# Input projection in two passes of four tiles, cache copies beside the first, samples routed from group 23

## The chip, the cores and the metric

The kernel runs on one core of one Trainium2 chip. The metric is the device time of one execution in microseconds (us), from the first to the last instruction with what lies around it; lower is better. Before the change it is 3765.6 us, the median of three runs (3765.25 to 3778.32).

## What is computed

One layer of a hybrid decoder, on 1024 prompt tokens and 64 sample tokens (8 sequences of 8), all in fp32, model width 1024:

```
z   = x @ w_in                      # 1024 x 2560: q, k, v, GLU value a, GLU gate g, 512 columns each
att = dilated sliding-window attention(q, k, v)      # 8 heads of 64
cnv = swish(LayerNorm(causal depthwise conv(a * sigmoid(g), width 31)))
x1  = LayerNorm(ALPHA * x + concat(att, cnv) @ w_out)
# PEER: 8 heads, query of 256, two sides of 128 keys
s   = (x1 @ w_query) against sub_keys;  top 16 of each side, top 16 of their 256 sums -> 128 experts per token
y   = LayerNorm(ALPHA * x1 + sum_k gate_k * gelu(x1 . expert_u[e_k]) * expert_v[e_k])
```

The samples attend to a cache of 2048 rows. The outputs also hold the new keys, values and GLU rows, and both caches (keys and values of 8 sequences) shifted by 8 rows, which are plain copies from DRAM to DRAM.

## The kernel before

**Tiles and stages.** The tokens are 9 tiles: 0 to 7 of 128 prompt tokens, and tile 8 (`PT`) of the 64 samples. Each engine runs its own hand-written program over stages `n` from -1 to 10; a stage has 32 groups `g`, a group four quarters `i`. In stage `n` the *front* of tile `m = n+1` runs (projection of later tiles, attention in groups 0 to 9, convolution, output projection in 11 and 12, LayerNorm in 13 and 14, queries, key scores and routing of 8 PEER heads from group 15 on), beside the *dots* of tile `n` (each: one gather of `expert_u` rows for 128 tokens by POOL, L574, and one multiply-and-sum on DVE, L1039) and the *values* of tile `n-1` (one gather of `expert_v` rows per token, L589, and four matmuls of it, L1376). A gather moves 512 KB. A dot of stage -1 can be made early, between the routing of heads of tile 0: 56 are (`EARLY_AT`); the other 72 of tile 0 are spread over stage 0. POOL runs no further ahead than its rings: 6 buffers for u, 8 for v.

**Routing.** One head is a fixed run of small DVE operations on 128 rows (`route_side` twice, `route_pairs`, `route_experts`). For prompt tiles head `h` begins at quarter 69 + 7h of the stage (group 17.25). For the samples (stage 7) head `h` takes the four quarters of group 24 + h; their queries and key scores run in groups 22 to 29.

**Projection.** `w_in` is read in steps of 128 columns (a, g four times, then k, q four times) and two v steps of 256 columns. Three passes go over all 18 steps (`PASSES`): the 128 tokens of tile 0; 512 tokens; the last 384 tokens with the 64 samples beside them (448 columns). A *unit* is 8 matmuls for one step (for v: one step and one tile). The profile shows each fp32 matmul as two records, so a unit is x16. Pass 0 (18 units, banks in rotation of 8) stands alone ahead of stage -1; the 24 units of pass 1 lie in stage -1 and the 24 of pass 2 in stage 0, in the groups that a table names, each behind the front's work of its group on PE:

```
UNIT_GROUP = [[2, 5, 8, 11, 14, 15] + [16 + j * 15 // 18 for j in range(18)], [j * 31 // 24 for j in range(24)]]
```

ACT copies each unit out of PSUM (`evacuate`) and then issues the weight load (L640, L642) of the step that takes the slot next (`w_ring`, 4 slots of 512 KB). Behind a g unit DVE multiplies a by sigmoid(g) (`gated`, L885) at the start of the next group, and ACT stores the product a group later (`gated_store`). In pass 0 q, the GLU rows and k of tile 0 stay in SBUF; later tiles go through scratch in DRAM. POOL's first value gather waits for all units, since the v ring lies where x and the weights lay.

**Queues.** SP issues, in this order: the first weights and x, constants; behind the third step from the end of pass 0 x of pass 1, `w_out`, the keys and LayerNorm rows; the first 8 cache copies (L458, 4080 KB each), the first near the end of pass 0 and one more after each head of stage -1; x of pass 2; the loads of front 1; the other 8 copies, one per head of stage 0; in stage 1 the projected outputs. A load of `wq` (1 MB per head) is issued by ACT.

**Value groups.** `v_group_at` (L425) makes the values of tile `n-1` run two groups behind (`V_LAG`), and `LAG` (L124) makes the 64 dots of the samples in stage 8 begin at group 2.

```
            k = GROUPS * (n - 1) + g - V_LAG
            return divmod(k, GROUPS) if 0 <= k < GROUPS * TILES else None
```

In stage 7 the samples' attention takes groups 0 to 17, their convolution rows 16 to 18, the output projection group 19, LayerNorm groups 20 and 21.

Of the kernel before, what the change touches and what calls it, by code (L numbers as in the profile page):

```python
# [10 lines left out]
ALU = mybir.AluOpType  # L11
# [3 lines left out]
P = 128  # L15
# [21 lines left out]
PH = 8  # L37
# [27 lines left out]
PASSES = ((0, P, 0), (P, 512, 0), (5 * P, 3 * P, NS))  # L65
# [3 lines left out]

def pass_tiles(p):
    t0, tn, sn = PASSES[p]
    return [(t0 + tn) // P - tn // P + j for j in range(tn // P)] + ([PT] if sn else [])
# [7 lines left out]

UNITS = []
for _p in range(3):
    for _s, (_k, _i) in enumerate(STEPS):
        UNITS += [(_p, _s, _k, _i, _t) for _t in (pass_tiles(_p) if _k == "v" else [None])]
UNIT_AT = [sum(1 for _u in UNITS if _u[0] < _p) for _p in range(4)]
FIRST_LOADS = UNIT_AT[1] - 6

def evac_ops(u):  # L90
    p, _, kind, _, _ = UNITS[u]
    return 2 if p == 2 and kind in "kq" else 1
# [7 lines left out]
for _p in range(3):  # L100
# [9 lines left out]
def unit(p, kind, i):  # L110
    return max(n for n, u in enumerate(UNITS) if u[0] == p and u[2:4] == (kind, i))

# [3 lines left out]
UNIT_GROUP = [[2, 5, 8, 11, 14, 15] + [16 + j * 15 // 18 for j in range(18)], [j * 31 // 24 for j in range(24)]]  # L116
assert all(len(UNIT_GROUP[p]) == UNIT_AT[p + 2] - UNIT_AT[p + 1] for p in range(2))
GATE_GROUP = [[UNIT_GROUP[p][2 * i + 1] for i in range(CT)] for p in range(2)]
# [5 lines left out]
LAG = 2  # L124
# [3 lines left out]

def units_at(m, g):  # L130
    return [UNIT_AT[m + 1] + j for j, at_ in enumerate(UNIT_GROUP[m]) if at_ == g] if m < 2 else []
# [41 lines left out]
def build(nc, I, O):  # L173
# [6 lines left out]
    with ctx:  # L180
# [85 lines left out]
        idf = small([P, SLOTS])  # L266
        dots = [small([P, SLOTS]) for _ in range(2)]
# [13 lines left out]
        assert base + taken[0] <= nc.sbuf_usable_end, (base + taken[0], nc.sbuf_usable_end)  # L281
# [6 lines left out]
        xT = [at(o_ring, [P, KD, P])] + [at(o_ring + U_RING * D * 4, [P, KD, 512])] * 2  # L288
# [7 lines left out]
        vs = at(o_l + 2 * D * 4 + 3 * 512 * 4, [NS, AW])  # L296
        conv_new = at(o_l + 2 * D * 4, [P, CT, NS])

# [18 lines left out]
        past_out = sem("past_out")  # L317
# [84 lines left out]
        q_free = {(p, i): 16 * (2 * (p - 1) + i // 2) for p in (1, 2) for i in range(CT)}  # L402
        glu_free = {(1, 0): 0, (1, 1): 0, (1, 2): 0, (1, 3): 16, (2, 0): 32, (2, 1): 16, (2, 2): 16, (2, 3): 80}
        GLU_FOUR, GLU_ALL = (32, 16, 16), (128, 64, 64)
# [19 lines left out]

        def v_group_at(n, g):  # L425
            k = GROUPS * (n - 1) + g - V_LAG
            return divmod(k, GROUPS) if 0 <= k < GROUPS * TILES else None
# [10 lines left out]
        def _(sp):  # L438
            sp.dma_start(w_ring[:, 0, :, :], I["w_in_t"][0]).then_inc(w_in_s[0], 16)
            sp.dma_start(xT[0][:, :, :], I["xT"][:, :, 0:P]).then_inc(xT_in[0], 16)  # L440
# [8 lines left out]
            sp.dma_start(xT[1][:, :, :], I["xT"][:, :, P:P + 512]).then_inc(xT_in[1], 16)  # L449
# [20 lines left out]
            def projected_loads():  # L470
                sp.wait_ge(proj_done, UNIT_AT[2])
                sp.dma_start(xT[2][:, :, 0:3 * P + NS], I["xT"][:, :, 5 * P:TOK]).then_inc(xT_in[2], 16)

            def projected_stores():
                sp.wait_ge(proj_evac, EVACS[-1])
                sp.dma_start(vs_o, vs[:, :]).then_inc(vs_out, 16)
                sp.dma_start(kT_o, kT[:, :, :]).then_inc(st_out, 16)
# [4 lines left out]
            def front_loads(m):  # L482
# [6 lines left out]
                if m == 1:  # L489
                    sp.wait_ge(past_out, 16)  # L490
# [70 lines left out]
            for i in range(3):  # L561
                sp.wait_ge(glu_out[i], GLU_ALL[i])
# [974 lines left out]
```

## Time and profile before

| | us |
|---|---|
| median of three runs | 3765.6 |
| the profiled execution, its own time | 3800.66 |
| span of the profiled execution | 3798.8 |

| engine | busy us | share |
|---|---|---|
| PE | 2453.4 | 65% |
| DVE | 2527.9 | 67% |
| POOL | 2128.8 | 56% |
| ACT | 387.7 | 10% |

The DMA engines moved 1394.91 MB, 367 GB/s over the span; the gathers' queue has 1140.99 MB of it. In the page's slices the DMA engines are busy 90% and more nearly everywhere, and TensorE's clock moves between its two levels. Times in the trace are counted from the span's start. A share of busy time is an average over stages with different limits, so the stretches are to be read one by one: in each, which wait ends last. The chain of waits names for each stretch the work that the rest waited for.

### The profile page before, as it was taken

The numbers are of one execution on the slowest core, as the hardware profiler recorded it, in microseconds if no ns is written. First come the engines' busy times: TensorE is split into PE (matmuls) and PEld (weight loads), VectorE is DVE, ScalarE is ACT, GpSimd is POOL, SyncE is SP. The second block draws the span as 40 slices with busy tenths as digits, with TensorE's granted clock in tenths as the row PEclk, the third lists the DMA queues.
The fourth block names the chain that finished last, engine by engine and source line by source line (L and its number), as shares of the span: only waits on it lengthen the run. The fifth ranks groups of instructions, "written<-read, shape, count | busy, mean of one in ns | idle before, by whom it ended". The sixth has DMA issues, their size and how long they took to land.

```text
span 3798.8 us, 32774 instructions
## 1 busy us (share of the span) xinstructions
PE 2453.4 (65%) x10596; PEld 1095.8 (29%) x10596; DVE 2527.9 (67%) x6632; ACT 387.7 (10%) x753; POOL 2128.8 (56%) x2180
## 2 busy tenths in 40 slices
PE   7894792666557655665666676767665655655558
PEld 5462371223123312222323132314231222321112
DVE  5288589768866886588668875887587434683331
ACT  2111211100110011001110011002100111000000
POOL 0042224666666665666566656666666545647665
PEclk8897895678668866887687767877787777778899
DMA  9998988999999998999899989999999999979998
GB/s 340 354 340 307 398 322 309 372 384 383 363 353 395 408 354 331 393 410 361 322 386 411 367 334 377 410 366 363 367 410 388 412 415 403 372 287 375 361 367 319
DMA packets 375450, 1394.91 MB, mean 367 GB/s; under 512 B 44712, under 2 KB 55592, under 8 KB 362856
## 3 DMA queue, kind: packets, MB, share of 16 engines
q0 software_dynamic: 313344, 1140.99, 78.4%
q1 hardware_dynamic: 40384, 143.03, 10.1%
q10 hardware_dynamic: 21552, 108.79, 7.4%
q8 instruction: 86, 1.41, 0.1%
q14 instruction: 84, 0.69, 0.0%
HBM read 1379.40 MB, written 80.18 MB: 384 GB/s over the span
## 4 chain that ended last, share of the span: by engine, by line
DVE 34%; PE 16%; issue 15%; POOL 14%; DMA 12%; another core or an unknown queue 7%; ACT 2%; ACTq 0%; SPq 0%; DVEq 0%; POOLq 0%
DVE t L1039 14%; POOL t L589 8%; DMA t<-in_expert_v,t 6%; PE psum L1376 6%; POOL t L574 6%; DMA t<-in_expert_u,t 5%; PE psum L1233 4%; DVE t L987 2%; DVE t L985 2%; DVE t L900 2%; DVE t L988 2%; DVE t L986 2%; PE psum L1277 1%; PE psum L1253 1%
## 5 line engine op out<-in xcount | busy, mean ns | idle before, releaser
L1376 PE MATMUL psum<-t,t 128*32 128x512 f32 x4352 | 1264.4, 782 | 797.5 <-DMA t<-in_expert_v,t 584.5
L574 POOL DMA_INDIRECT t<-in_expert_u,t x1088 | 1062.9, 977 | 976.0 <-DVE t L1039 510.3
L589 POOL DMA_INDIRECT t<-in_expert_v,t x1088 | 1065.6, 979 | 675.5 <-issue 298.1
L1039 DVE CUSTOM_DVE_ANT_0 t<-psum,t 128x1024 f32<-128x1024 f32 x928 | 1116.8, 1220 | 337.9 <-DMA t<-in_expert_u,t 294.4
L1376 PEld LDWEIGHTS psum<-t,t 128*32 128x32 f32 x4352 | 258.2, 129 | 1608.0 <-issue 1536.9
L1332 PE MATMUL psum<-t,t 128*128 128x128 f32 (+1 forms) x2304 | 302.5, 292 | 34.4 <-issue 22.9
L1332 PEld LDWEIGHTS psum<-t,t 128*128 128x128 f32 x2304 | 291.2, 207 | 87.2 <-issue 72.8
L1039 DVE CUSTOM_DVE_ANT_0 t<-t,t 128x1024 f32<-128x1024 f32 x160 | 194.3, 1223 | 155.6 <-DMA t<-in_expert_u,t 153.8
L1233 PE MATMUL psum<-t,t 128*128 128x128 f32 (+2 forms) x768 | 258.8, 496 | 7.0 <-DMA t<-in_xT 6.3
L900 DVE SCALAR_TENSOR_TENSOR t<-t,t,t 128x128 f32<-128x128 f32 x840 | 237.8, 345 | 0.5 <-issue 0.4
L1253 PE MATMUL psum<-t,t 64*128 64x512 f32 (+3 forms) x192 | 119.7, 748 | 100.2 <-issue 53.4
L1277 PE MATMUL psum<-t,t 128*128 128x64 f32 x576 | 106.8, 350 | 112.3 <-issue 99.1
L1233 PEld LDWEIGHTS psum<-t,t 128*128 128x128 f32 x768 | 132.6, 203 | 118.4 <-issue 111.2
L1277 PEld LDWEIGHTS psum<-t,t 128*128 128x128 f32 x576 | 98.4, 259 | 184.9 <-issue 165.6
L1313 PE MATMUL psum<-t,t 128*128 128x512 f32 (+1 forms) x288 | 134.0, 620 | 3.4 <-ACT t L694 3.4
L1055 DVE SCALAR_TENSOR_TENSOR t<-t,t 128x128 f32<-128x128 f32 (+1 forms) x288 | 80.5, 281 | 83.4 <-PE psum L1376 55.9
L984 DVE MAX8 t<-t 128x8 f32<-128x128 f32 (+3 forms) x216 | 72.3, 335 | 94.2 <-ACT t L738 57.2
L730 ACT ACTIVATE t<-psum 128x256 f32<-128x256 f32 (+1 forms) x72 | 26.7, 371 | 882.1 <-remote 788.0
L1344 PE MATMUL psum<-t,t 128*128 128x128 f32 (+1 forms) x288 | 63.8, 359 | 79.2 <-ACT t L730 46.6
L933 DVE CUSTOM_DVE_ANT_0 t<-psum,t 128x128 f32<-128x128 f32 (+7 forms) x64 | 48.1, 752 | 97.1 <-PE psum L1253 47.0
L1344 PEld LDWEIGHTS psum<-t,t 128*128 128x128 f32 (+1 forms) x288 | 49.6, 237 | 145.7 <-issue 73.5
L1039 DVE DVE_READ_ACCUMULATOR2_ANT t<- 128x1 f32 x1088 | 89.5, 82 | 0.0
(140 smaller groups left out, 1805.7 us busy)
## 6 DMA issues: line engine op xcount, KB each, us to landing
t<-in_wq_t ACTq DMA_DIRECT2D x72, 1024.0 KB
out<-in_cache_k_win SPq DMA_DIRECT2D x8, 4080.0 KB
out<-in_cache_v_win SPq DMA_DIRECT2D x8, 4080.0 KB
t<-in_w_in_t ACTq DMA_DIRECT2D x44, 512.0 KB, 8.0
t<-in_kc_t SPq DMA_DIRECT2D x8, 2560.0 KB, 15.1
t<-in_vc_t SPq DMA_DIRECT2D x8, 2560.0 KB
t<-in_expert_u,t POOLq DMA_INDIRECT x1088
t<-in_expert_v,t POOLq DMA_INDIRECT x1088
```

Of the source, the lines that this page charges most:

```text
L574: pool.indirect_dma_start(u_buf[:, k % U_RING, :], None, I["expert_u"][0], bass.IndirectOffsetOnAxis(ap=idn[t % 2][:, s:s + 1], axis=0)).t ...
L589: pool.indirect_dma_start(v_buf[:, k % V_RING, :], None, I["expert_v"][0], bass.IndirectOffsetOnAxis(ap=idT[t % 3][:, tau:tau + 1], axis=0 ...
L900: dve.scalar_tensor_tensor(dst, src, w, dst, ALU.mult, ALU.add).then_inc(cv, 1)
L1039: dve.tensor_tensor_reduce(out=u_buf[:, k % U_RING, :], in0=x1P if banked else x1[t % 3][:, :], in1=u_buf[:, k % U_RING, :], scale=1.0, sc ...
L1055: dve.scalar_tensor_tensor(zt[:, k % Z_RING, 0:w, :], iota[:, :].unsqueeze(1).broadcast_to([P, w, 32]), float(g), c3, ALU.is_equal, ALU.mu ...
L1233: last = pe.matmul(dst[:, 0:tn + sn], w_ring[:, r, k, :], xT[p][:, k, 0:tn + sn], start=(k == 0), stop=(k == KD - 1))
L1253: last = pe.matmul(bank[2 + half][:, 0:w], qT[r:r + E, c, :], kT[r:r + E, c, half * 512:half * 512 + w], start=True, stop=True)
L1277: last = pe.matmul(bank[2][:, 0:E], pT[:, j * P:(j + 1) * P], v[:, j, h * E:(h + 1) * E], start=(j == 0), stop=(j == m))
L1313: last = pe.matmul(bank[3 - half][0:rows(m), :], mixedT[:, k, 0:rows(m)], w_out[:, k, half * 512:(half + 1) * 512], start=(k == 0), stop=( ...
L1332: last = pe.matmul(bank[2 + h % 2][:, side * r:(side + 1) * r], wq[:, h % 2, k, side * KEYC:(side + 1) * KEYC], x1T[:, k, 0:r], start=(k = ...
L1344: last = pe.matmul(bank[4 + h % 2][0:r, side * NK:(side + 1) * NK], qh[:, h % 2, side * r:(side + 1) * r], skT[:, 2 * h + side, :], start= ...
L1376: last = pe.matmul(bank[half][32 * j:32 * j + 32, :], zt[:, (GROUPS * t + g) % Z_RING, j, :], v_buf[:, k % V_RING, half * 512:(half + 1) * ...
```

## The change

**Two passes.** `PASSES = 2`, each of 512 tokens (four tiles). Pass 0 has 24 units (16 of 512 columns, 8 v units) and still stands ahead of stage -1. In pass 1 each a, g, k and q step is two units, one of 512 columns and one of the 64 samples, whose x has a buffer of its own (`xTs`, on the place of tile 7's v; so the last v unit of tile 7 goes to the end); with v 42 units, in groups 4 to 52 counted from the start of stage -1. The weights are read twice, not three times.

**Tile 0's rows.** In pass 0 ACT writes q twice (tile 0's part to `qT`, all to the store), DVE multiplies the GLU rows of tile 0 a second time into `gl`, and all four tiles go to scratch; the store of tile 0's last 30 rows goes away. The samples' GLU rows are made in place in `gluS` and stored from there by SP in stage 1.

**Copies.** Nine of the 16 cache copies are issued beside pass 0 (after units 4, 6, ... 20), four in stage -1, three in stage 0. x of pass 1 is issued by ACT behind its last work of pass 0.

**Samples.** Their queries begin at group 21 and head `h` of their routing at quarter 92 + 9h/2 (group 23 on); the first LayerNorm operations move two quarters up. `HOLD, HELD`: in groups 18 and 19 of stage 7 no value group runs, and from there the values are four groups behind. `LAG` is 4. The value stream ends at group 3 of stage 10, and the last LayerNorm follows it there.

```diff
-PASSES = ((0, P, 0), (P, 512, 0), (5 * P, 3 * P, NS))
+HALF = SEQ // 2
+HT = HALF // P
+PASSES = 2
...
+        _tiles = range(HT * _p, HT * (_p + 1)) if _k == "v" else [None]
+        _tiles = ([PT] if _p and _k == "v" else []) + list(_tiles) + ([PT] if _p and _k != "v" else [])
+        UNITS += [(_p, _s, _k, _i, _t) for _t in _tiles]
...
+FIRST_LOADS = 2
+COPY_AT = [4, 6, 8, 10, 12, 14, 16, 18, 20]
...
-UNIT_GROUP = [[2, 5, 8, 11, 14, 15] + [16 + j * 15 // 18 for j in range(18)], [j * 31 // 24 for j in range(24)]]
-GATE_GROUP = [[UNIT_GROUP[p][2 * i + 1] for i in range(CT)] for p in range(2)]
+STEP_GROUP = [4, 8, 12, 15, 17, 19, 21, 23, 25, 27, 29, 31, 33, 36, 39, 42]
+UNIT_GROUP = [_g for _g in STEP_GROUP for _ in range(2)] + [43 + _j for _j in range(10)]
+GATE_GROUP = [STEP_GROUP[2 * _i + 1] for _i in range(CT)]
...
-LAG = 2
+LAG = 4
...
+HOLD, HELD = GROUPS * (PT - 2) + 18, 2
+SAMPLE_ROUTE = [92 + 9 * _h // 2 for _h in range(8)]
+SAMPLE_QUERY = 21
...
+        def v_number(n, g):
+            at_ = GROUPS * (n - 1) + g
+            if HOLD <= at_ < HOLD + HELD:
+                return None
+            return at_ - V_LAG - (HELD if at_ >= HOLD else 0)
...
-            for i in range(PH):
-                if i:
-                    sp.wait_ge(sm_done, i)
-                else:
-                    sp.wait_ge(proj_done, UNIT_AT[1] - 2)
+            for i, u in enumerate(COPY_AT):
+                sp.wait_ge(proj_done, u)
                 copy_cache(i)
...
-            projected_loads()
+            for i in range(4):
+                sp.wait_ge(sm_done, 2 * i + 1)
+                copy_cache(len(COPY_AT) + i)
...
+            act.dma_start(xT[:, :, :], I["xT"][:, :, HALF:SEQ]).then_inc(xT_in[1], 16)
...
+                if p == 0:
+                    step(dve.tensor_tensor(gl[:, i, PAST:], dst[:, 0:P], gate[:, 0:P], ALU.mult))
+                dve.tensor_tensor(dst, dst, gate, ALU.mult).then_inc(glu_done, 1)
+                if p:
+                    dve.wait_ge(proj_evac, EVACS[unit(p, "g", i, PT)])
+                    dve.tensor_tensor(gluS[:, i, :, PAST:], gluS[:, i, :, PAST:], sigS[:, i % 2, :].rearrange("p (b t) -> p b t", b=NB),
+                                      ALU.mult).then_inc(gluS_done, 1)
...
-                if g >= 24:
-                    if i < 2:
-                        route_side(PT, g - 24, i)
-                    elif i == 2:
-                        route_pairs(PT, g - 24)
-                    else:
-                        route_experts(PT, g - 24)
+                for h in range(PH):
+                    at_ = 4 * g + i - SAMPLE_ROUTE[h]
+                    if at_ in (0, 1):
+                        route_side(PT, h, at_)
+                    if at_ == 2:
+                        route_pairs(PT, h)
+                    if at_ == 3:
+                        route_experts(PT, h)
...
+                if u == UNIT_AT[1] + 1:
+                    pe.wait_ge(xT_in[2], 16)
...
+                if tile is None:
+                    x_, w = xT, HALF
+                elif tile < PT:
+                    x_, w = xT[:, :, (tile - HT * p) * P:(tile - HT * p + 1) * P], P
+                else:
+                    x_, w = xTs, NS
```

Where the instructions stand, at three places. First PE at the start of stage -1: L1253 (L1291 in the changed kernel) are the scores of a head, L1266 (L1304) the transposes of its weights, L1277 (L1315) its values, L1233 (L1271) a projection unit; t_122 and, in the changed kernel, t_121 are x, t_123 the weights. Before:

```order
L1253 MATMUL psum<-t_50,t_53 128x128 [waits const_in,proj_evac]
L1266 MATMUL psum<-t_94,t_56 128x128 [waits exp_done]
L1253 MATMUL psum<-t_50,t_53 128x128 [waits sm_done]
L1277 MATMUL psum<-t_51,t_57 128x64 [waits sm_done,pT_ready]
L1266 MATMUL psum<-t_94,t_56 128x128 [waits pT_ready,exp_done]
L1253 MATMUL psum<-t_50,t_53 128x128 [waits att_done,sm_done]
L1233 MATMUL psum<-t_122,t_123 128x512 [waits proj_evac,w_in0,xT_in1]
```

The changed kernel, from the fourth head's scores on:

```order
L1291 MATMUL psum<-t_50,t_53 128x128 [waits att_done,sm_done]
L1315 MATMUL psum<-t_51,t_57 128x64 [waits att_done,sm_done,pT_ready]
L1304 MATMUL psum<-t_94,t_56 128x128 [waits pT_ready,exp_done]
L1291 MATMUL psum<-t_50,t_53 128x128 [waits att_done,sm_done]
L1271 MATMUL psum<-t_121,t_123 128x512 [waits proj_evac,w_in0,xT_in1]
L1271 MATMUL psum<-t_121,t_123 128x512 x7
L1271 MATMUL psum<-t_122,t_123 128x64 [waits proj_evac,w_in0,xT_in2]
L1271 MATMUL psum<-t_122,t_123 128x64 x7
L1315 MATMUL psum<-t_51,t_57 128x64 [waits att_done,sm_done,pT_ready]
```

The first unit stood behind the scores of the third head; now it stands behind those of the fifth, and a unit of 64 columns with the same weights follows it. Second, PE in the first groups of stage 0. Before, a unit follows the scores in each of these groups:

```order
L1253 MATMUL psum<-t_50,t_53 128x256 [waits att_done,sm_done]
L1233 MATMUL psum<-t_122,t_123 128x448 [waits proj_evac,w_in1]
L1233 MATMUL psum<-t_122,t_123 128x448 x7
L1277 MATMUL psum<-t_51,t_57 128x64 [waits att_done,sm_done,pT_ready]
L1277 MATMUL psum<-t_51,t_57 128x64
L1266 MATMUL psum<-t_94,t_56 128x128 [waits pT_ready,exp_done]
L1266 MATMUL psum<-t_94,t_56 128x128
L1253 MATMUL psum<-t_50,t_53 128x256 [waits att_done,sm_done]
L1233 MATMUL psum<-t_122,t_123 128x448 [waits proj_evac,w_in2]
```

The changed kernel:

```order
L1271 MATMUL psum<-t_121,t_123 128x512 [waits proj_evac,w_in0]
L1271 MATMUL psum<-t_121,t_123 128x512 x7
L1271 MATMUL psum<-t_122,t_123 128x64 [waits proj_evac,w_in0]
L1271 MATMUL psum<-t_122,t_123 128x64 x7
L1315 MATMUL psum<-t_51,t_57 128x64 [waits att_done,sm_done,pT_ready]
L1315 MATMUL psum<-t_51,t_57 128x64
L1304 MATMUL psum<-t_94,t_56 128x128 [waits pT_ready,exp_done]
L1304 MATMUL psum<-t_94,t_56 128x128
L1291 MATMUL psum<-t_50,t_53 128x256 [waits att_done,sm_done]
L1315 MATMUL psum<-t_51,t_57 128x64 [waits att_done,sm_done,pT_ready]
```

Two heads in three now have no unit behind their scores, and the third has two units. Third, POOL in stage 7, the changed kernel around the held groups (L601 gathers u, L616 v; before, u and v take turns there):

```order
L601 DMA t_86<-in_expert_u,t_96 128x1024 [waits a_dot]
L616 DMA t_87<-in_expert_v,t_99 128x1024 [waits pv]
L601 DMA t_86<-in_expert_u,t_96 128x1024 [waits a_dot] x8
L601 DMA t_86<-in_expert_u,t_96 128x1024 [waits a_dot,a_route]
L616 DMA t_87<-in_expert_v,t_99 128x1024 [waits pv_first]
```

Eight v gathers are gone from between the u gathers; they come after the rest of the stream, in stage 8.

## Rows read from the trace of the kernel before

**Rows 1.** The page: its first line, one group of gathers, one group of loads

```profile
span 3798.8 us, 32774 instructions
...
L574 POOL DMA_INDIRECT t<-in_expert_u,t x1088 | 1062.9, 977 | 976.0 <-DVE t L1039 510.3
...
t<-in_w_in_t ACTq DMA_DIRECT2D x44, 512.0 KB, 8.0
```

**Rows 2.** Windows: us from:to, length, busy of five engines, clock, DMA share, GB/s

```profile
54.00:178.00 124.00, 99.18 (x265) 49.88 (x265) 21.80 (x70) 28.39 (x61) 0.00 (x0) 0.83 1.02 352
178.00:334.00 156.00, 113.90 (x505) 77.80 (x504) 139.35 (x387) 13.94 (x32) 58.57 (x62) 0.88 0.89 319
334.00:495.00 161.00, 127.07 (x360) 67.05 (x360) 95.02 (x260) 33.66 (x69) 39.24 (x40) 0.86 1.00 382
495.00:617.00 122.00, 78.73 (x432) 62.00 (x430) 114.49 (x348) 15.76 (x39) 31.31 (x34) 0.83 0.78 284
1400.00:1800.00 400.00, 244.02 (x1024) 102.53 (x1023) 294.30 (x769) 39.78 (x74) 255.47 (x264) 0.77 0.97 374
```

**Rows 3.** Chain of waits, 0 to 200 us (start us, us, what)

```profile
6.29 5.48 PE psum L1233 x32
...
65.77 9.78 PE psum L1233 x16
...
98.36 8.70 PE psum L1233 x16
...
123.19 6.87 PE psum L1233 x16
130.06 6.88 PE psum L1313 x16
...
143.10 1.97 PE psum L1321 x8
...
178.57 0.22 DVE t L984
...
188.37 0.18 DVE t L1016
```

**Rows 4.** Timeline of PE, 40 to 200 us (start us, us, what, idle before)

```profile
49.62 3.72 PE L1231 MATMUL psum<-t,t 128*128 128x256 f32 x16 [1.15 <-DMA t<-in_w_v_t]
53.81 0.48 PE L1253 MATMUL psum<-t,t 64*128 64x128 f32 x2 [0.47 <-ACT t L614]
```

**Rows 5.** Chain of waits, 333 to 620 us

```profile
334.59 1.12 DVE t L897 x4
...
386.14 1.09 PE psum L1277 x4
...
393.21 1.08 PE psum L1277 x4
...
429.26 0.44 PE psum L1294 x4
...
495.54 0.30 DVE t L984
...
616.53 1.12 DVE t L897 x4
```

**Rows 6.** DMA issues, all of the run: count, KB each, median us to landing

```profile
t<-in_xT SPq DMA_DIRECT2D x1, 2048.0 KB, 15.4
t<-in_xT SPq DMA_DIRECT2D x1, 1792.0 KB, 19.2
```

**Rows 7.** Timeline of PE at 3271 us, queries of the 64 samples

```profile
3271.51 6.09 PE L1332 MATMUL psum<-t,t 128*128 128x64 f32 x47
```

**Rows 8.** Windows of the samples' routing

```profile
3260.00:3300.00 40.00, 27.88 (x157) 17.65 (x158) 16.46 (x40) 1.31 (x4) 24.62 (x25) 0.71 0.99 375
3340.00:3380.00 40.00, 23.54 (x120) 11.20 (x120) 37.66 (x118) 1.31 (x4) 21.30 (x23) 0.77 0.89 323
3400.00:3420.00 20.00, 7.02 (x34) 1.54 (x34) 13.95 (x42) 4.42 (x7) 3.78 (x5) 0.59 0.28 98
```

More of the change, by code:

```diff
@@ L99 @@
 _uses, _last = [0] * 4, [None] * 4
-for _p in range(3):
+for _p in range(PASSES):
     for _s, _slots in enumerate(STEP_SLOTS):
@@ L476, in projected_stores @@
                 sp.dma_start(vs_o, vs[:, :]).then_inc(vs_out, 16)
+                sp.wait_ge(gluS_done, CT)
+                for c in range(CT):
+                    sp.dma_start(glus_o[:, c, :].rearrange("p (b t) -> p b t", b=NB), gluS[:, c, :, PAST:]).then_inc(glus_out, 16)
                 sp.dma_start(kT_o, kT[:, :, :]).then_inc(st_out, 16)
@@ L519, in cache_copies @@
             def cache_copies():
-                for h in range(PH):
-                    sp.wait_ge(sm_done, PH + h + 1)
-                    copy_cache(PH + h)
+                for i in range(len(COPY_AT) + 4, 2 * NB):
+                    sp.wait_ge(sm_done, PH + 2 * (i - len(COPY_AT) - 4) + 1)
+                    copy_cache(i)
             def store_y(t):
@@ L801, in sample_front @@
                     x1_transposed(PT)
-                if 22 <= g < 30:
-                    for h in (g - 22 - g % 2, g - 21 - g % 2):
-                        if g % 2:
-                            score_copy(PT, h)
-                        else:
-                            query_copy(PT, h)
+                heads, second = sample_heads(g)
+                for h in heads:
+                    if second:
+                        score_copy(PT, h)
+                    else:
+                        query_copy(PT, h)
                 if g == 31:
@@ L848, in _ @@
                         sample_front(g)
-                    if n == -1 and g == 1:
-                        act.wait_ge(glu_done, CT)
-                        act.dma_start(glu_d[:, :, P:P + PAST], gl[:, :, P:P + PAST]).then_inc(past_out, 16)
-                    if n < 1:
-                        for i in range(CT):
-                            if g == GATE_GROUP[m][i] + 2:
-                                gated_store(m + 1, i)
+                    for i in range(CT):
+                        if GROUPS * m + g == GATE_GROUP[i] + 2:
+                            gated_store(1, i)
                     for u in units_at(m, g):
@@ L1440, in sample_front @@
                     x1_transposes(PT)
-                if 22 <= g < 30:
-                    for h in (g - 22 - g % 2, g - 21 - g % 2):
-                        if g % 2:
-                            key_scores(PT, h)
-                        else:
-                            queries(PT, h)
+                heads, second = sample_heads(g)
+                for h in heads:
+                    if second:
+                        key_scores(PT, h)
+                    else:
+                        queries(PT, h)
             def front(m, g):
```

148 lines of the change are left out of this document (71 added, 77 removed).

## The prediction

> **What bounds the kernel now.** I read the page first, then windows by stage, then the chain of waits at their borders, then PE's timeline where the chain ran through projection units. The page gives the span, 3798.8 us, and the two gather streams of 1088 gathers each [rows 1]; the windows show four stretches ahead of a long steady part, cut at events of the chain:
>
> - 0 to 53.8: pass 0 alone. PE's first scores start at 53.81, right behind the last v unit [rows 4].
> - 53.8 to 178.6 (124.8 us): front of tile 0, until DVE starts the first head's routing [rows 3]. PE is busy 99 of 124 us, DVE 22 [rows 2], and the chain goes through units [rows 3].
> - 178.6 to 334.6 (156.0): routing with early dots, up to the first taps of stage 0 [rows 3, 5]. DVE is busy 139 of 156: DVE bounds it [rows 2].
> - 334.6 to 495.5 (160.9): front of tile 1 until its routing [rows 5]. PE 127 of 161, DVE 95 [rows 2].
> - 495.5 to 616.5 (121.0): its routing and the remaining dots; DVE 114 of 122, DMA share only 0.78 [rows 2, 5].
> - 616.5 on: one gather of u and one of v per token slot. DMA share 0.97 at 374 GB/s, no engine above 74% [rows 2]. This is bound by DMA, and its DMA work is the same in both kernels, except for where the samples' end leaves gaps.
>
> So the DMA engines are full on average, but ahead of 616.5 the chain does not run through them: the share is 1.02 at 54 to 178 because copies were put there, not because someone waits for them. From this follows my reading: the time is the moment at which stage 1 can start, plus a fixed DMA-bound rest. Copies must only be out of the way by then.
>
> **Part 1, pass 0 (+100 us).** Before, its end is at 53.8. Now: the first matmul starts at 6.3 with 1 MB loaded [rows 3]; 1.5 MB more of x at 352 GB/s [rows 2] adds 4.5, so 10.8. 16 units of 512 columns at 6.87 us, measured where PE ran without a break [rows 3]: 110. Eight v units at 3.72 [rows 4]: 30. The first v load can be issued only behind unit 13, about 14 us before it is needed; I allow 3. Sum 153.8, against 53.8: +100. Beside it lie nine copies and the constants. Weights have four slots, 27 us ahead, against 8.0 us median to landing [rows 1], and 76 GB/s of demand: hidden, if the copies do not crowd them out (rival below). The doubled q copies (ACT) and GLU products (DVE) are 0.4 to 0.7 us beside units of 6.87: nothing. DVE's 124 taps for tile 0 move under pass 0.
>
> **Part 2, front of tile 0 (-29).** Before 124.8 with nine units in groups 2 to 16. Now four steps (groups 4, 8, 12, 15), each 6.87 us plus a unit of 64 columns. The row for 64 columns is 47 records in 6.09 us, 130 ns each, so 16 records are 2.1 us [rows 7]; a step is 9.0. After attention pauses a 512-column unit took 9.78 and 8.70 instead of 6.87 [rows 3], so 2 more at groups 4 and 8. Heads without a unit go at some 2.2 us (an estimate: 124.8 less nine units and the pieces below leaves about that). Step by step: five heads 10; wait for x of pass 1, whose 2048 and 1792 KB took 15.4 and 19.2 us to land [rows 6] and which is issued when pass 0 ends: 17 less 10 is 7; step 11; four heads 9; step 11; from the end of group 8's unit (107.0) to the x1 transposes (143.1) before took 36, one unit of 6.87 in it [rows 3]: the unit at group 12 now covers the LayerNorm gap of 6.2 (136.9 to 143.1) and costs 9.0, so 32; transposes 2; queries 3.6; step 9; sigmoid and product 1.3, for which DVE waits in group 16 ahead of the routing. Sum 96: -29. Ends for this part: -40 (x lands in time, no slow units) and -10 (x 15 us late, units at half clock).
>
> **Part 4, front of tile 1 (-24).** Before 160.9. Group pitch with no unit is 7.07 us (386.14 to 393.21), DVE's own pace [rows 5]. Now group 0 has no unit but DVE's work keeps it at 13; groups 1, 4, 7: 2.9 of attention plus 9.0, 11.9 each; groups 2, 3, 5, 6 at 7.07. Sum 77 to group 8, before 95 (334.59 to 429.26 [rows 5]). Groups 8 to 17 before took 66. Now: convolution LayerNorm uncovered 8, its neighbours 1, step 9, two halves of the output projection 14, seven v units, 26 less the 6 that the LayerNorm gap hides, transposes, scores and copies 3: 55, and queries 3.6: 59. With 1 us of slow clock in all: 137. -24. The GLU products leave this stage; in it DVE waited for units that are in the sum already. Ends: -36 and -10.
>
> **Part 5, routing of tile 1 (0)**: DVE-bound with DMA idle a fifth of the time, before and after. The 10.5 MB of weights saved and five copies fewer in stage 0 fall into DMA time that nobody waits for: nothing. If stage 0 were DMA-bound, 10.5 MB at 374 GB/s would be 28 us (rival).
>
> **Part 6, samples (-9).** At 3300 to 3410 DVE is busy 37.7 of 40 us [rows 8]: eight heads at about 10 us (178.57 to 188.55 [rows 3]) plus four dots each. DMA falls to 0.89 and, at 3400 to 3420, to 0.28 while PE waits in order for the last routing [rows 8]. Lost there: about 20 us of DMA time in all. Head 0 moves into group 23, which DMA bounds, so the DVE-bound stretch is a head shorter: -9. The eight held v gathers make groups 18 and 19 shorter by 11 us (8 times 0.524 MB at 374 GB/s) and are paid again in stage 8, where DMA is full: zero. They do not lift PE's wait for the last head. `LAG` 4 moves dots within a DMA-bound stage: zero. Ends: -20 (all lost DMA time) and +6 (with the holds, DVE waits for the output projection while only u gathers are under way).
>
> **Sum.** 100 - 29 - 24 - 9 = +38. The profiled execution took 3800.66 us, 35 above the median 3765.6; I carry the difference over: 3803.6, rounded 3803 (+1.0%).
>
> **Rivals.**
> - *DMA decides after all (faster).* If the stretches up to 616 are paced by DMA (share 1.02 and 1.00 in two of four [rows 2]), copies put under a PE-bound pass and 10.5 MB less pay: -28 from the bytes and -9 at the end, about 3729. It decides if heads and units in 54 to 178 waited for loads. Against it: the chain there alternates PE and DVE, and the window's PE is busy 80%. Chance 0.12.
> - *Most of the pass is won back (no change).* x lands in time (-7), no slow units (-5), first gathers at once (-6), stage 0 at its lower end (-12), all idle DMA time at the samples filled (-11): +38 becomes about -3, and around half of these gives +15. 3765 to 3782. Chance 0.17.
> - *Copies crowd out the weights (slower still).* By 154 us the kernel now wants 62 MB (nine copies of 4.18, weights 11.5, output weights and keys 7, x 2.4, stores and small ones 3.5); at 352 GB/s [rows 2] that takes 176. If the weights wait their turn by bytes, pass 0 ends at 176: +22, 3825; with x of pass 1 late as well, 3835. For it: the sum of bytes. Against it: beside running copies weights landed in 8.0 us median [rows 1]. The Trainium skill, "DMA: Bandwidth & Descriptors", section Queues, rings and completion order, says each engine takes turns between queues by packet, which would keep ACT's weights moving past SP's backlog; by that rule this rival gets less. Chance 0.14.
> - That the samples' stream or the copies are not moved as said: the order of instructions leaves no room for that.
>
> **Chances.** Forecast 0.57, its own range 3784 to 3822. About 0.5%, 19 us, is what a measurement of this kernel can tell from no change. Faster by more: 0.12, the first rival. Within: 0.17 of the second and 0.01 of the forecast's edge, 0.18. Slower: 0.70. The range takes in the second and most of the third rival and a part of the first: 3752 to 3832.
>
> **What would show it.** Right: first scores at 150 to 157 us, PE without gaps before; first u gather (before at 188.8, right behind the first head [rows 3]) at 250 to 265; first taps of stage 1 at 655 to 675 instead of 616.5; steady stages unchanged; DMA share in the second tile's front well under 1. DMA at the samples' end still with one hole of some 15 us. Wrong: taps of stage 1 ahead of 630 (parts 2 and 4 won more), or scores behind 165 (crowding), or steady stages of another length, which would mean that the rest was not fixed.

## The result and the profile after

The changed kernel takes 3821.6 us (median of four runs, 3819.95 to 3831.56) against 3772.0 for the kernel before in the same comparison: ratio 1.0133, interval 1.0109 to 1.0157. It is 49.6 us slower. Forecast were 3803 and +38, range 3752 to 3832.

The profiled execution of the changed kernel took 3819.95 us, 19 more than that of before (3800.66). The medians differ by 50; so the profiled pair shows 30 us less than the medians, a difference between two executions and not of the change: the profiled execution of before is itself 29 us above the median of its kernel. Where it sits is seen when the span is cut at the events of the prediction. The page first, its first line and the DMA volume:

```profile
span 3818.1 us, 32732 instructions
...
DMA packets 375914, 1384.89 MB, mean 363 GB/s; under 512 B 48504, under 2 KB 56312, under 8 KB 363576
```

The volume fell by the forecast 10 MB (1394.91 before), and the mean rate fell with it (367 before). That bytes ahead of stage 1 buy nothing is shown below, by the runs without the copies. The chain of waits of the changed kernel, 0 to 750 us, rows of pass 0 and the two stage starts (L929 are the first taps of a stage, L897 before):

```profile
10.20 111.86 PE psum L1271 x256
122.06 27.64 PE psum L1269 x128
...
417.30 1.11 DVE t L929 x4
...
671.48 1.11 DVE t L929 x4
```

Pass 0 is one unbroken block of PE up to 149.7; the first taps of stage 1 stand at 671.5, before at 616.5 [rows 5]. The timeline of DVE gives the two starts of routing (L1017 is its first operation, L984 before):

```profile
264.09 0.29 DVE L1017 MAX8 t<-t 128x8 f32<-128x128 f32 x1 [1.36 <-ACT t L774]
```

```profile
550.33 0.30 DVE L1017 MAX8 t<-t 128x8 f32<-128x128 f32 x1 [6.41 <-ACT t L774]
```

| stretch | before, us | after, us | difference | forecast |
|---|---|---|---|---|
| pass 0, to the first scores | 53.8 | 150.2 | +96.4 | +100 |
| front of tile 0 | 124.8 | 113.9 | -10.9 | -29 |
| routing of tile 0 | 156.0 | 153.2 | -2.8 | 0 |
| front of tile 1 | 160.9 | 133.0 | -27.9 | -24 |
| routing of tile 1 | 121.0 | 121.2 | +0.2 | 0 |
| sum, to stage 1 | 616.5 | 671.5 | +55.0 | +47 |
| rest | 3182.3 | 3146.6 | -35.7 | -9 |

The first five rows are the forecast's and hold, with one miss of 18 us. The last is mostly not the change's: see the experiment with both kernels on one chip below. The windows of the changed kernel answer to [rows 2] (the same columns):

```profile
0.00:150.00 150.00, 139.49 (x384) 73.52 (x384) 47.41 (x136) 15.76 (x30) 0.20 (x4) 1.00 0.94 331
150.00:264.00 114.00, 79.96 (x270) 47.77 (x270) 15.15 (x51) 24.89 (x60) 0.00 (x0) 0.76 0.99 327
264.00:417.00 153.00, 103.23 (x500) 68.25 (x498) 140.68 (x392) 12.54 (x33) 60.32 (x62) 0.85 0.80 277
417.00:550.00 133.00, 100.80 (x360) 60.68 (x361) 91.26 (x251) 22.95 (x59) 39.06 (x40) 0.78 0.82 302
550.00:671.00 121.00, 51.70 (x333) 48.31 (x331) 113.69 (x343) 12.95 (x28) 31.01 (x33) 0.71 0.69 230
```

Both routing stretches have DVE at 92 and 94% (89 and 94% before) and last within 3 us as long as before, though PE fell from 79 to 52 us of work in the second: PE's work was moved from beside a bound engine to ahead of everything. DMA has more idle time than before in these three stretches (0.80, 0.82, 0.69 against 0.89, 1.00, 0.78), and neither routing is clearly shorter for it.

**Where the front of tile 0 missed.** The chain of waits of the changed kernel, 150 to 280 us:

```profile
150.58 27.12 DMA t<-in_xT
177.74 10.46 PE psum L1271 x32
...
214.37 16.04 PE psum L1351 x32
230.41 8.61 PE psum L1271 x32
...
239.42 1.28 ACT L755
...
244.54 1.98 PE psum L1359 x8
...
247.19 6.42 PE psum L1370 x32
```

x of pass 1 took 27.1 us to land, not 17: the last copies of pass 0 ran beside it. SP had issued the last two at 131.7 and 146.6 us, a copy lands 21 to 54 us after its issue, and the four copies of stage -1 were issued only from 196.7 us on, when x had landed. PE had finished its scores at 161.2 and stood 16.6 us, not 7. The output projection took 16.0, not 14, and the queries 6.4, not 3.6, at a granted clock of 0.87 and 0.58 (1.00 in pass 0): before the queries PE had stood 5.5 us. In the kernel before a projection unit stood behind that pause, and the queries took 3.57 us. And the step at group 12 (230.4 to 239.0) did not cover the LayerNorm gap: ACT, which works in order, copies that step out of PSUM before it takes the LayerNorm's root (L755), so the gap of 5.5 us to 244.5 stood behind the step. DVE waited for that root 8.6 us (its waits, 150 to 268 us):

```profile
DVE t L1010 <- ACT t L755: 8.6, 1, 8.6
```

ACT's copies of the step start at 237.3 and 239.0, its root at 239.4. That its order is the cause is read from the code and these times; no run moved the copy alone.

### The profile page after: what moved, and what is told of

Its sections match the earlier page's. It is cut to its first block, busy times and chain, and to the rows that moved or that the text cites. A ratio compares the mean times of both kernels' runs of the same rounds, so it can differ in the third digit from the quotient of the medians.

```text
span 3818.1 us, 32732 instructions
## 1 busy us (share of the span) xinstructions
PE 2474.6 (65%) x10596; PEld 1097.9 (29%) x10596; DVE 2526.4 (66%) x6632; ACT 377.7 (10%) x740; POOL 2140.2 (56%) x2180
## 3 DMA queue, kind: packets, MB, share of 16 engines
q1 hardware_dynamic: 43504, 141.07, 10.2%
## 4 chain that ended last, share of the span: by engine, by line
DVE 33%; PE 18%; issue 13%; POOL 13%; DMA 12%; another core or an unknown queue 9%; ACT 2%; ACTq 0%; SPq 0%; DVEq 0%; POOLq 0%
DVE t L1072 14%; POOL t L616 7%; PE psum L1414 6%; POOL t L601 6%; DMA t<-in_expert_v,t 5%; PE psum L1271 5%; DMA t<-in_expert_u,t 5%; DVE t L1020 2%; DVE t L1018 2%; DVE t L1021 2%; DVE t L932 2%; DVE t L1019 2%; PE psum L1291 2%; PE psum L1315 1%
## 5 line engine op out<-in xcount | busy, mean ns | idle before, releaser
L601 POOL DMA_INDIRECT t<-in_expert_u,t x1088 | 1072.5, 986 | 1000.1 <-DVE t L1072 441.3
L616 POOL DMA_INDIRECT t<-in_expert_v,t x1088 | 1067.4, 981 | 660.6 <-issue 302.1
L1370 PE MATMUL psum<-t,t 128*128 128x128 f32 (+1 forms) x2304 | 320.1, 302 | 20.8 <-issue 19.2
L1370 PEld LDWEIGHTS psum<-t,t 128*128 128x128 f32 x2304 | 307.9, 217 | 74.2 <-issue 72.2
L1271 PE MATMUL psum<-t,t 128*128 128x512 f32 (+1 forms) x768 | 267.5, 510 | 36.2 <-DMA t<-in_xT 26.8
L1291 PE MATMUL psum<-t,t 64*128 64x512 f32 (+3 forms) x192 | 117.1, 733 | 108.1 <-issue 56.8
L1271 PEld LDWEIGHTS psum<-t,t 128*128 128x128 f32 x768 | 133.8, 200 | 171.3 <-issue 144.3
L1315 PE MATMUL psum<-t,t 128*128 128x64 f32 x576 | 101.3, 336 | 99.9 <-issue 90.9
L1351 PE MATMUL psum<-t,t 128*128 128x512 f32 (+1 forms) x288 | 135.2, 625 | 11.2 <-ACT t L730 7.3
L1382 PE MATMUL psum<-t,t 128*128 128x128 f32 (+1 forms) x288 | 63.8, 358 | 118.7 <-ACT t L766 104.8
L1315 PEld LDWEIGHTS psum<-t,t 128*128 128x128 f32 x576 | 92.3, 245 | 164.9 <-issue 150.9
L1017 DVE MAX8 t<-t 128x8 f32<-128x128 f32 (+3 forms) x216 | 72.3, 335 | 97.4 <-ACT t L774 46.6
```

Of the source, the lines that this page charges most:

```text
L601: pool.indirect_dma_start(u_buf[:, k % U_RING, :], None, I["expert_u"][0], bass.IndirectOffsetOnAxis(ap=idn[t % 2][:, s:s + 1], axis=0)).t ...
L616: pool.indirect_dma_start(v_buf[:, k % V_RING, :], None, I["expert_v"][0], bass.IndirectOffsetOnAxis(ap=idT[t % 3][:, tau:tau + 1], axis=0 ...
L1271: last = pe.matmul(dst[:, 0:w], w_ring[:, r, k, :], x_[:, k, :], start=(k == 0), stop=(k == KD - 1))
L1291: last = pe.matmul(bank[2 + half][:, 0:w], qT[r:r + E, c, :], kT[r:r + E, c, half * 512:half * 512 + w], start=True, stop=True)
L1315: last = pe.matmul(bank[2][:, 0:E], pT[:, j * P:(j + 1) * P], v[:, j, h * E:(h + 1) * E], start=(j == 0), stop=(j == m))
L1351: last = pe.matmul(bank[3 - half][0:rows(m), :], mixedT[:, k, 0:rows(m)], w_out[:, k, half * 512:(half + 1) * 512], start=(k == 0), stop=( ...
```

## Experiments

Two of the twelve runs are the changed kernel and the kernel before as they are; the other ten move one or two of three parts: the copies, the samples' end, and where the projection units stand (e9 also where the GLU products stand). e1 to e4 ran on one chip and e5 to e12 on another; the kernel before takes the same on both (medians 3607 to 3610 us). Which chip the first comparison ran on is not known, nor so whether the chip makes its difference; "the first chip" stands for it. There the steady stages are 7% longer, so only ratios are compared with it. Stage 1's start is each kernel's first tap of that stage, in DVE's timeline; start and rest are of one profiled execution each. The start differs by up to 6 us between executions that are the same up to there (668.8 in e3, 675.0 in e11; 616.4 to 619.3 in e7, e12 and e4), and the rest by up to 14 between executions that are the same from there on (2980.1 in e5, 2993.8 in e11).

| kernel | ratio to before | interval | stage 1 starts, us | rest, us |
|---|---|---|---|---|
| e12 before | 1.0006 | 0.9996 to 1.0016 | 617.3 | 2993.4 |
| e11 changed | 1.0146 | 1.0130 to 1.0161 | 675.0 | 2993.8 |
| e1 before, no copies | 0.9995 | 0.9986 to 1.0004 | 617.8 | 2980.1 |
| e2 changed, no copies | 1.0095 | 1.0082 to 1.0109 | 654.9 | 2989.8 |
| e3 changed, samples as before | 1.0139 | 1.0123 to 1.0154 | 668.8 | 2984.6 |
| e4 before, samples as changed | 1.0002 | 0.9993 to 1.0011 | 619.3 | 2990.0 |
| e5 changed, five copies first | 1.0144 | 1.0128 to 1.0160 | 674.8 | 2980.1 |
| e6 before, units late | 0.9956 | 0.9942 to 0.9970 | 601.7 | 2986.9 |
| e7 before, route 23, no hold | 0.9987 | 0.9978 to 0.9996 | 616.4 | 2980.1 |
| e8 = e6 and e7 | 0.9934 | 0.9921 to 0.9948 | 600.7 | 2981.6 |
| e9 = e8, products later | 0.9899 | 0.9884 to 0.9914 | 582.8 | 2981.8 |
| e10 changed, steps late | 1.0079 | 1.0065 to 1.0093 | 648.6 | 2988.5 |

### Both kernels on one chip

The changed kernel and the kernel before, unaltered, both on the second of the two chips.

> The changed kernel on the chip of the experiments, where the steady stages are 7% shorter than on the first chip. Theory A (an added path of some 50 us that does not depend on DMA speed): 1.0135 to 1.0145 of before, the same 50 us. Rival (a loss in proportion to the DMA-bound rest): 1.0133 and 48 us.

> The kernel before, for a profile on the chip of the experiments. Theory A: stage 1 starts at 616 to 618 as on the first chip, although the steady stages are 7% shorter; the rest is 2980 to 2990.

The kernel before, its first line, and from DVE's timeline the row at the start of stage 1 (the first taps):

```profile
span 3610.7 us, 32774 instructions
```

```profile
617.27 0.85 DVE L897 TENSOR_SCALAR t<-t,t 128x128 f32<-128x128 f32 x3
```

The changed kernel, the same two:

```profile
span 3668.9 us, 32732 instructions
```

```profile
675.05 0.59 DVE L929 TENSOR_SCALAR t<-t,t 128x128 f32<-128x128 f32 x2
```

The span shrank by 188 us against the first profile of the kernel before (the medians by 163), and stage 1 of the kernel before still starts at 617, as on the first (616.5): the way there does not depend on the DMA rate that sets the rest. Between the kernels the start differs by 57.7 us and the rest by 0.4, so the 36 us by which the rest seemed shorter on the first chip were a difference of two executions. A steady stage, from the first taps of stage 1 to those of stage 2, lasts 356.5 us before and 356.2 changed. The ratio is the first chip's within its interval; it can't tell theory A from its rival (1.0133 lies in its interval too), but the two starts and the equal rests can. The rest of the kernel before, 2993.4, lies just outside the 2980 to 2990 expected.

### Without the copies

Both kernels, all 16 cache copies left out (their outputs are not written), and the wait for them at the end:

```diff
             def copy_cache(i):
-                new, old = ((kc_o, I["cache_k_win"]), (vc_o, I["cache_v_win"]))[i % 2]
...
+                pass
...
-            sp.wait_ge(cache_out, 16 * 2 * NB)
```

> The kernel before without its 16 cache copies (66.8 MB, left out of the computation). Theory A (the way to stage 1 is set by PE and DVE, the rest is a fixed stretch bound by gathers, copies lie in DMA time that nobody waits for): 0 to 15 us faster than before (3757 to 3772), and nearly all of that ahead of stage 1. Theory B (DMA volume decides everywhere): 66.8 MB at 374 GB/s is 178 us, so at least 100 us faster.

> The changed kernel without its 16 cache copies (left out of the computation). Theory A: the 27 us in which x of pass 1 landed shrink to about 10, the first gathers come a little sooner: 12 to 22 us faster than the changed kernel, 3800 to 3810, still 0.8% slower than before. Pass 0 ends at 150 as with copies. Theory B: at least 100 us faster. A third reading (copies slowed pass 0 itself): first scores ahead of 145.

This is the sharpest test of the first rival. 66.8 MB less, 4.8% of all bytes, changed the kernel before by nothing: 0.9995. Stage 1 starts at 617.8. From 54 to 179 us the DMA share is 0.33 without the copies, 1.03 with them (e12), and the routing begins at 180.0 and 179.3. DMA time ahead of stage 1 was free there, although its share was above 1. In the changed kernel the copies do cost: without them it is 1.0095 instead of 1.0146, 18 us, and stage 1 starts 20 us sooner than in e11, 14 sooner than in e3, which ran on the same chip as e2. Pass 0 ends at 150.7, so they did not slow the pass (it ends at 150.2 to 151.3 in four other executions with copies, at 153.3 in e11); the front of tile 0 took 97.2 us instead of 114.9. One of its DMA issue rows says why, the x of pass 1, from the changed kernel without copies:

```profile
t<-in_xT ACTq DMA_DIRECT2D x1, 2048.0 KB, 10.4
```

and with them (e11; in e3, which ran on the same chip as e2, it took 27.0):

```profile
t<-in_xT ACTq DMA_DIRECT2D x1, 2048.0 KB, 27.9
```

Theory A gave 12 to 22 us for this and was right on the mechanism and the size. What is left, 1.0095 or 34 us, is the change without any copies: a pass longer by some 90 us ahead of everything, less what the fronts behind it give back.

### Five copies beside pass 0

```diff
-COPY_AT = [4, 6, 8, 10, 12, 14, 16, 18, 20]
+COPY_AT = [4, 6, 8, 10, 12]
...
-            for i in range(4):
-                sp.wait_ge(sm_done, 2 * i + 1)
+            for i in range(8):
+                sp.wait_ge(sm_done, i + 1)
```

> The changed kernel with five copies beside pass 0 instead of nine, one behind each of the eight heads of stage -1, three in stage 0. Theory A (x of pass 1 waits behind copies that are still running when pass 0 ends): x lands about 10 us sooner, route of tile 0 starts 8 to 12 us sooner than in the changed kernel, 0.25% faster than it, still about 1.011 of before. Rival (x is slow by its own shape, 2 KB rows): no change, 1.0135.

```profile
t<-in_xT ACTq DMA_DIRECT2D x1, 2048.0 KB, 19.7
```

x landed 8 us sooner and the routing of tile 0 began at 256.0 instead of 268.2, as theory A said; but the time did not follow (1.0144). The routing of tile 0 then lasted 165.3 us instead of 154.4. The waits of DVE inside it, here and in the unaltered changed kernel:

```profile
DVE t L1072 <- DMA t<-in_expert_u,t: 13.8, 3, 7.7
```

```profile
DVE t L1072 <- DMA t<-in_expert_u,t: 4.3, 2, 2.3
```

Those waits are 9.5 of the 11 us: the copies were pushed under the first gathers of u, and the dots waited for those instead. Nor did x land as soon as without copies (10.4): here three copies were issued at 152.0, 155.1 and 157.5 us, just behind x at 151.4. A copy is free where nobody waits for a load; neither of these two placements of 13 copies is free. The forecast of a gain failed.

### The samples' part alone, in both directions

The changed kernel with the samples as before (e3), and the kernel before with the samples as changed (e4). The core of both, from the changed kernel's side:

```diff
-LAG = 4
+LAG = 2
-HOLD, HELD = GROUPS * (PT - 2) + 18, 2
+HOLD, HELD = GROUPS * (PT - 2) + 18, 0
-SAMPLE_ROUTE = [92 + 9 * _h // 2 for _h in range(8)]
-SAMPLE_QUERY = 21
+SAMPLE_ROUTE = [96 + 4 * _h for _h in range(8)]
+SAMPLE_QUERY = 22
```

> The changed kernel with the samples' end as it was before (routing one head per group from group 24, queries from 22, no held value groups, dots two groups behind): the projection part alone. Theory A with my price of 9 us for the samples: 3831, and by the medians of the two kernels (55 us lost ahead of stage 1, 50 in all) some 5: 3827. Rival: the held groups and the earlier LayerNorm cost time: 3800 to 3815.

> The kernel before with the samples' part of the change alone (routing from group 23, two held value groups, dots four groups behind). Theory A: 5 to 9 us faster than before, 3763 to 3767, ratio about 0.998. Rival (holding v only moves work and the wait of PE for the last head stays): within 2 us of before.

> The kernel before with the samples routed from group 23 but no held value groups and dots two groups behind. If the held groups gained 3 us where they stood and cost 11 at the tail, and the earlier routing gained the rest: 4 to 8 us faster than before, ratio 0.998. Rival (without the hold the first samples' queries come too late, DVE waits in group 23): within 2 us.

e7 is e4 with `HELD` 0 and `LAG` 2. The rival holds for e4: 1.0002, no gain, and e3 is 1.0139 against 1.0146, where theory A wanted a loss. The reading of the line that closes the samples' routing (the softmax of the gates; its last start is the samples') splits this. The kernel before, then e4, then e7:

```profile
L1022 DVE TENSOR_TENSOR t<-t x9: 283/284/286, 332.9 to 3251.7; 128x128 f32<-128x128 f32 x8, 64x128 f32<-64x128 f32 x1
```

```profile
L1035 DVE TENSOR_TENSOR t<-t x9: 277/285/286, 335.6 to 3240.2; 128x128 f32<-128x128 f32 x8, 64x128 f32<-64x128 f32 x1
```

```profile
L1035 DVE TENSOR_TENSOR t<-t x9: 277/284/286, 332.2 to 3241.2; 128x128 f32<-128x128 f32 x8, 64x128 f32<-64x128 f32 x1
```

From the start of stage 1 to there: 2634.4 before, 2620.9 with all of the samples' part, 2624.8 without the hold. These three alone would give 9.6 us to routing from group 23, but the same code varies by as much, and all twelve traces together say less:

| samples' part | runs | stage 1 to that line, us (mean) | that line to the end, us (mean) |
|---|---|---|---|
| as before | e12, e1, e6, e3 | 2625.7 to 2634.4 (2630) | 354.4 to 359.0 (356) |
| from group 23, no hold | e7, e8, e9 | 2624.8 to 2625.9 (2625) | 355.3 to 356.5 (356) |
| as changed | e2, e4, e5, e10, e11 | 2614.6 to 2622.2 (2620) | 365.5 to 371.6 (368) |

So routing from group 23 gains about 5 us, where the prediction had 9, and the held groups with `LAG` 4 gain 5 more and cost 12 at the end; no run separates these two. Why the hold shortens its own stretch by so little is not shown. By medians e7 is 0.9987, 4.7 us, at the lower edge of what was expected; e4 lost that again. The DMA hole at the end of the routing became shallower with routing from group 23, not with the hold: from 12 us before that line to 8 after it the DMA share is 0.29 to 0.32 in the runs with the samples as before, 0.58 in e7, e8 and e9, and 0.58 to 0.62 with the hold. This stretch in the kernel before:

```profile
3240.00:3260.00 20.00, 6.51 (x34) 1.47 (x34) 14.50 (x44) 4.42 (x7) 3.12 (x4) 0.58 0.31 106
```

The hold adds nothing here, and the end behind it is 12 us longer.

### Units behind the start of routing

The same principle turned round: the kernel before, with fewer units ahead of the routings.

```diff
-UNIT_GROUP = [[2, 5, 8, 11, 14, 15] + [16 + j * 15 // 18 for j in range(18)], [j * 31 // 24 for j in range(24)]]
+UNIT_GROUP = [[3, 6, 10, 14] + [17 + j * 13 // 20 for j in range(20)], [2, 4, 6, 8, 10, 12, 14, 16, 17, 18, 18, 19, 20, 20, 21, 21, 22, 23, 24, 25, 26, 27, 28, 29]]
```

> The kernel before with its pass 1 and 2 units moved behind the start of routing (4 instead of 9 units ahead of it in stage -1, 8 instead of 14 in stage 0). Theory A (units ahead of the routing are on the path at 6 to 9 us each, units beside the DVE-bound routing are free while PE has room): stage 1 starts 30 to 50 us sooner, ratio 0.987 to 0.992. Rival 1 (DMA volume decides): no change. Rival 2 (PE, now full beside the routing, delays queries and so the routing): the fronts get shorter and the routing stretches as much longer, within 5 us of before.

> Both of the two changes above together. If the parts are independent, as a sum of a path ahead of stage 1 and a fixed rest would have it: the gains of the two add, 0.985 to 0.990. Rival (the rest is not fixed, a sooner stage 1 is given back): less than the first alone.

The fronts became shorter by 27 and 15 us (119.9 to 92.5, 161.9 to 147.3), and the routings longer by 22 and 7; pass 0 ended 3 us sooner in this execution. Stage 1 starts 15.6 us sooner, ratio 0.9956. Both theory A and its rival of a full PE were half right; the direction is A's, the size is not (0.987 to 0.992 expected). The waits of DVE in tile 0's routing, 179 to 335 us of the kernel before, then 149 to 327 of e6 (waiting line, releaser, sum in us, times, longest):

```profile
DVE t L885 <- ACT t L634: 13.4, 1, 13.4
DVE t L1039 <- DMA t<-in_expert_u,t: 8.5, 2, 6.6
```

```profile
DVE t L885 <- ACT t L634: 14.8, 2, 13.8
DVE t L1039 <- DMA t<-in_expert_u,t: 14.2, 8, 6.6
DVE t L984 <- ACT t L738: 4.0, 1, 4.0
```

L885 is the GLU product; it stands at the start of a group in DVE's program and waits for the sigmoid of the unit, and so for PE. In the kernel before that wait ended at 178.7, just ahead of the first head of routing (179.3), and counts in the front; in e6 the first head starts at 149.1 and the wait follows it. So some 14 of the 27 and of the 22 us are one wait that changed sides, and both stretches together tell the true gain: 275.1 before, 270.1 in e6. The rest of the longer routing is later u gathers (6) and the copy of the key scores (4). With routing from group 23 added (e8) the gains add: 0.9934 against 0.9956 and 0.9987, though the 0.985 to 0.990 expected, built on e6's, was missed. In e8 the products (now L898) also hold DVE in the front of tile 1, 328 to 473 us:

```profile
DVE t L898 <- ACT t L649: 37.9, 4, 13.2
```

The next run moves the products:

```diff
-                                if g == GATE_GROUP[m][j] + 1:
+                                if g == GATE_GROUP[m][j] + 2:
...
-                            if g == GATE_GROUP[m][i] + 2:
+                            if g == GATE_GROUP[m][i] + 3:
```

> The kernel with units late and routing from group 23, and each GLU product of DVE and its store one group further behind its unit. In the trace with units late DVE waited 26 us for sigmoids in the stretch around the first routing. Theory A (those waits stretch the routing): 6 to 15 us faster than that kernel, ratio to before 0.989 to 0.992. Rival (queries that PE brings late stretch it): no change, 0.993.

0.9899: 13 us below e8 and the fastest of all, 36 us below the kernel before. The waits of DVE in tile 0's routing, 147 to 323 us, and the largest in the front of tile 1, 322 to 443 (L1052 is the dot, L997 the first operation of a head, L753 the copy of the key scores that it waits for, L978 waits for the output projection):

```profile
DVE t L1052 <- DMA t<-in_expert_u,t: 19.7, 13, 3.6
DVE t L997 <- ACT t L753: 7.6, 1, 7.6
```

```profile
DVE t L978 <- PE psum L1325: 8.4, 2, 6.3
```

In the routing the product's wait is gone and others took its place, so it stayed at 175.6 us (177.8 in e8). The front of tile 1 lost its product waits and fell from 145.5 to 121.6, with the routing behind it 12 longer. So the expected saving came, but not in the place that theory A had named: the waits for products that were on the path were those in the front of stage 0.

### Steps late in the changed kernel

```diff
-STEP_GROUP = [4, 8, 12, 15, 17, 19, 21, 23, 25, 27, 29, 31, 33, 36, 39, 42]
+STEP_GROUP = [6, 13, 17, 18, 19, 21, 22, 23, 25, 26, 27, 29, 30, 31, 36, 40]
```

> The changed kernel with two projection steps instead of four ahead of the routing in stage -1 and two instead of four ahead of it in stage 0. Theory A (an exposed step costs 9 to 11 us): both fronts 15 to 20 us shorter, the routing of tile 0 stretched by 5 to 15, stage 1 some 15 to 25 us sooner, ratio 1.008 to 1.010. Rival (the loss is pass 0 and DMA, not the exposed steps): within 4 us of the changed kernel, 1.013.

1.0079, 24 us below the changed kernel. Stage 1 starts 26.4 sooner: front of tile 0 83.8 instead of 114.9, its routing 169.6 instead of 154.4, front of tile 1 122.9 instead of 131.5. Half of the change's loss can be had back by the place of the steps alone. Against the kernel before on the same chip (e12), e10 has pass 0 92 us longer, the fronts 36 and 39 shorter and the first routing 14 longer: 31 us later at stage 1.

## Why the prediction was right

**The frame.** That the time is the start of stage 1 plus a fixed rest is shown: rests lie between 2980.1 and 2993.8 us in twelve executions while stage 1 starts anywhere from 582.8 to 675.0, and the ratios follow the starts: 92 us between the ends of that range, 89 us between the times of e9 and e11 by their ratios. That bytes ahead of stage 1 were worth nothing in the kernel before is shown by e1. The rival "DMA decides" is refuted.

**Part 1** (+100): +96.4. PE started at 10.2 (10.8 forecast) and ran its units at 111.9 and 27.6 us; the allowance of 3 for the first v load was not needed. Pass 0 of the kernel before was not wholly on the path: its end lies between 53.8 and 64.2 us in five executions with the same units, and the routing begins at 178.5 to 181.3 in all of them. How the sum splits between parts 1 and 2 depends on the execution.

**Part 2** (-29, ends -40 and -10): -10.9, at the end of its range. The step that failed is the wait for x, sized from two landings of 15.4 and 19.2 us [rows 6] of which neither had a queue of cache copies beside it (issued at 30.6 and 298.0 us, copies at 37.7 and then from 61.4 to 138.4); 27.1 was measured, 10 us of the 18. That the copies lag was in the third rival's sum: in its first 150 us the kernel moved 50 MB (331 GB/s) of the 62 counted there, and what was left ran beside x. Second, "the unit at group 12 now covers the LayerNorm gap": it did not, 5.5 us, because ACT's order was not looked at. The output projection and the queries, at the lower clock, took 5 more, and small pieces gave 2 to 3 back. e2 bears the split out: with x in time the stretch is 97.2, where the forecast without its 7 us of wait is 89, so 8 of the 18 have nothing to do with x. A step at full clock took 8.6, not 9.0: the row that priced the 64-column unit had a granted clock of 0.89 (3271.5 to 3277.6 us), and 8.61 less 16 records of 0.429 leaves 109 ns for each of its records, not 130.

**Parts 3 and 5** (0, 0): -2.8 and +0.2.

**Part 4** (-24): -27.9.

**Part 6** (-9): the routing from group 23 gained about 5, not 9; and that the eight held v gathers cost nothing failed. Priced as 11 us shorter where they are held, they were 5 shorter there and cost 12 at the end (with `LAG` 4). In sum -4.7 without the hold and +0.7 with it, by the ratios, where -9 was forecast.

**Sum.** +38 forecast, +49.6 measured: 8 of the difference are ahead of stage 1, where part 2's miss is partly made up by parts 1, 3 and 4, and about 10 are the samples. That is more than the 11.6 between forecast and medians; the ratio's interval, 1.0109 to 1.0157, is 41 to 59 us and takes in both, and on the second chip the ratio 1.0146 is 53. Of the signs named in advance, the first u gather came at 274.4, outside 250 to 265, by part 2's miss. First scores (150.2), taps (671.5) and the DMA share of the second front (0.82) came as said, and equal stages are shown on one chip; the hole at the samples' end, said to be some 15 us, was 8 (a share of 0.60 over 20 us). Of the third rival, the crowding of pass 0 by copies did not happen, pass 0 was 4 us shorter than forecast; what it said of a late x did. The Trainium skill, "DMA: Bandwidth & Descriptors", section Queues, rings and completion order, has the engines take turns between queues by packet; pass 0's weights, which nothing slowed, agree with that, and the x load, 10.4 us alone and 27.9 beside the copies, shows that the turns can still cost more than double.

## What to carry to other kernels

A pass ahead of everything pays its whole length. A projection is cheap only beside a stretch that another engine bounds, so in this kernel the first pass should be the smallest that lets that engine begin, and weights read once more cost nothing while no engine waits for DMA there. Before bytes are saved or moved, take them all away once and see whether the time moves. And a load on which the next stage waits should not run beside copies that nobody waits for, whether they are issued ahead of it or just behind it.

## What the runs showed of the hardware

- A DMA share of 1.02 in the windows of a stretch said nothing of whether the stretch was bound by DMA: without 66.8 MB of copies the share from 54 to 179 us fell from 1.03 to 0.33 (e12, e1), and the routing behind it began no sooner (179.3, 180.0).
- A load of 2048 KB on ACT's queue took 10.4 us alone and 27.1 to 27.9 us in the changed kernel, with cache copies of 4080 KB still on SP's queue; in e5, with the next copies issued just behind it, 19.7.
- With PE busy without a break for 140 us (pass 0) the granted clock was 1.00, the upper of its two levels; in the stretch after it, with pauses of 0.4 to 17 us, 0.76 on the mean. Behind a pause of 5.5 us the queries (32 records) ran at 0.58 and took 6.42 us; in the kernel before they took 3.57, behind a projection unit.
- The first comparison and the experiments, on two chips that agree with each other, differed by 7% in the steady stages, at DMA rates of 374 to 377 and 400 to 404 GB/s in the same window of 400 us, and by 1 us in the start of stage 1 of the kernel before. The window of the kernel before in e12, against [rows 2]:

```profile
1400.00:1800.00 400.00, 278.35 (x1167) 118.77 (x1161) 318.28 (x824) 49.01 (x89) 276.79 (x288) 0.81 1.02 403
```
